# The end of a 31-tap convolution module: per-tile operand copies on two queues, squares summed on TensorE, and an earlier table load

## The reference, cut to what matters

```python
def conformer_conv(h, w1, b1, dw, dwb, ln_g, ln_b, w2, b2):
    u = h @ w1 + b1
    a, g = jnp.split(u, 2, axis=-1)
    u = a * jax.nn.sigmoid(g)
    u = dwconv(u, dw) + dwb          # depthwise, 31 taps
    u = jax.nn.silu(layernorm(u, ln_g, ln_b))
    return u @ w2 + b2
```

## Time and profile before

| what | value |
|---|---|
| time, median of 3 runs | 3130.01 us (3128.34 to 3136.8) |
| the profiled execution | 3120.8 us |
| its span | 3118.7 us |
| PE busy | 2922.0 us, 94% of the span |
| DVE, ACT, POOL busy | 65%, 38%, 12% |
| granted PE clock, mean | 0.97 |

### The profile page before, as it was taken

How to read it: one execution, slowest core, us unless ns; L and a number is a source line. 1 busy time by engine, 2 the same in 40 slices (tenths; PEclk the granted TensorE clock), 3 DMA queues, 4 the chain that set the end, 5 groups by cost and what they waited for, 6 DMA issues and landing times.

```text
span 3118.7 us, 41453 instructions
## 1 busy us (share of the span) xinstructions
PE 2922.0 (94%) x17128; PEld 2494.5 (80%) x17128; DVE 2011.5 (65%) x3228; ACT 1186.1 (38%) x1927; POOL 359.0 (12%) x540
## 2 busy tenths in 40 slices
PE   7998999889988989999998899999999999998898
PEld 7997899879977767888864578887887888787898
DVE  6776677758765657666663576667667664454665
ACT  5443444544443434333231442233224223343544
POOL 0000101000013221000122100001010000144000
PEclk9999999989989999999999899999999999999999
DMA  6544566436646543444455134443444442366453
GB/s 222 167 165 142 168 231 224 144 127 226 226 154 137 103 71 112 155 146 142 142 152 153 56 127 155 142 147 120 145 144 133 145 145 99 85 113 93 123 182 132
DMA packets 361756, 451.78 MB, mean 145 GB/s; under 512 B 12400, under 2 KB 332176, under 8 KB 361568
## 3 DMA queue, kind: packets, MB, share of 16 engines
q1 hardware_dynamic: 326208, 328.72, 32.2%
q0 software_dynamic: 35200, 119.82, 15.2%
q10 hardware_dynamic: 160, 0.59, 0.1%
HBM read 438.67 MB, written 1.05 MB: 141 GB/s over the span
## 4 chain that ended last, share of the span: by engine, by line
PE 77%; DVE 12%; ACT 5%; issue 3%; DMA 2%; POOL 1%; SPq 0%; DVEq 0%; ACTq 0%; POOLq 0%
PE ps L1011 23%; PE ps L1012 22%; PE ps L1013 22%; DVE MX L1533 2%; DVE lo L1479 2%; DVE lo L1482 2%; PE ps L1176 1%; ACT hi L1208 1%; PE ps L1167 1%; PE ps L1032 1%; PE ps L1034 1%; PE ps L1033 1%; DVE NB L1491 1%; DMA NB<-in_na_rpb 1%; PE ps L1076 1%
## 5 line engine op out<-in xcount | busy, mean ns | idle before, releaser
L1011 PE MATMUL ps<-XN,hi 128*128 128x256 f32 (+1 forms) x3008 | 1021.3, 340 | 80.4 <-DVE XN L1505 32.4
L1012 PE MATMUL ps<-XN,hi 128*128 128x256 f32 (+1 forms) x3008 | 1007.0, 335 | 0.0
L1013 PE MATMUL ps<-XN,lo 128*128 128x256 f32 (+1 forms) x3008 | 1006.3, 335 | 0.0
L1011 PEld LDWEIGHTS ps<-XN,hi 128*128 128x128 f32 x3008 | 582.5, 194 | 167.7 <-DVE XN L1505 39.7
L1013 PEld LDWEIGHTS ps<-XN,lo 128*128 128x128 f32 x3008 | 581.9, 193 | 54.5
L1012 PEld LDWEIGHTS ps<-XN,hi 128*128 128x128 f32 x3008 | 583.0, 194 | 52.8
L1479 DVE TENSOR_TENSOR lo<-raw,hi 128x1024 fp32r<-128x1024 f32 (+1 forms) x313 | 385.2, 1231 | 289.8 <-ACT hi L1208 288.0
L1533 DVE CUSTOM_DVE_ANT_0 MX<-MW,C 128x1024 bf16<-128x1024 f32 x384 | 485.7, 1265 | 41.0 <-DMA MW<-in_mod_w 34.3
L1208 ACT ACTIVATE hi<-raw 128x1024 fp32r<-128x1024 f32 (+1 forms) x313 | 326.1, 1042 | 440.7 <-PE ps L1013 436.4
L1482 DVE TENSOR_TENSOR lo<-raw,hi 128x1024 fp32r<-128x1024 f32 (+1 forms) x313 | 381.1, 1218 | 0.0
L1013 PE MATMUL ps<-H,lo 128*128 128x512 f32 (+1 forms) x1024 | 371.2, 363 | 0.0
(11 more groups left out here) (224 smaller groups left out, 3420.3 us busy)
## 6 DMA issues: line engine op xcount, KB each, us to landing
raw<-in_mlp_w SPq DMA_DIRECT2D x128, 1024.0 KB, 4.9
MW<-in_mod_w POOLq DMA_DIRECT2D x192, 512.0 KB, 3.8
raw<-in_ffn_w_in SPq DMA_DIRECT2D x44, 1024.0 KB, 5.0
raw<-in_attn_w_in SPq DMA_DIRECT2D x36, 1024.0 KB, 4.9
raw<-in_na_wqkv SPq DMA_DIRECT2D x24, 1024.0 KB, 5.7
raw<-in_ffn_w_out SPq DMA_DIRECT2D x16, 1024.0 KB, 5.1
raw<-in_mlstm_w_in SPq DMA_DIRECT2D x12, 1024.0 KB, 5.1
raw<-in_cv_w SPq DMA_DIRECT2D x12, 1024.0 KB, 5.6
```

What stands on the lines that cost most here:

```text
L1011: e.matmul(out, whi, xhi, start=first, stop=False)
L1012: e.matmul(out, whi, xlo, start=False, stop=False)
L1013: i = e.matmul(out, wlo, xhi, start=False, stop=last)
```

## The change

Three edits, all between the last product of the first matrix and the first product of the second one.

1. For c = 3 the step `cv_spread` is replaced by two steps `cv_spread_one`, one for tile 6 and one for tile 7, each right behind its `cv_a`. Each of them is carried out by two engines: POOL issues the copies of channel groups 0 and 1, SP those of groups 2 and 3, eight DMAs each, of 32 partitions x 572 columns. The convolutions of tiles 6 and 7 wait for the two halves of their own tile. Four semaphores are added.
2. The load of the logarithm and exponential table moves from behind convolution 7 to ahead of convolution 4.
3. `by_pool` goes from 2 to 1: POOL adds nothing, and PE takes in the squares of tiles 1 to 7 one by one.

```diff
         def evac_a(t, b, u):
             p.do("cv_a", 2 * c + t, t, b, u)
-            if t == 1:
+            if c == 3:
+                p.do("cv_spread_one", 6 + t)
+            elif t == 1:
                 p.do("cv_spread", c)
...
         for k in (2 * c - 2, 2 * c - 1):
             if k >= 0:
+                if k == KT - 4:
+                    p.do("tables", LNEXP)
                 convolve(k)
     for k in (KT - 2, KT - 1):
         convolve(k)
     p.sa_user = "cv_summed"
-    p.do("tables", LNEXP)
     p.do("cv_mean", p.bank_use[6], p.rs_user)
     for k in range(KT):
         p.do("cv_center", k, p.norms)
-        p.square(k, 512, 2, "CV")
+        p.square(k, 512, 1, "CV")
         p.flush()
...
+def spread_one(e, m, k, g, signal, name):
+    for i in range(4):
+        e.dma_start(m.UX[32 * i:32 * i + 32, k // 2 % 2, g, k % 2, 0:572],
+                    m.U[32 * g:32 * g + 32, k % 4, i:i + 572]).then_inc(*signal.says((name, k)))
...
 def sync(e, w, m, p, T, sig):
...
+    def cv_spread_one(k):
+        w.wait_ge(("cv_u", k), ("conv", 3))
+        for g in range(2, 4):
+            spread_one(e, m, k, g, sig[f"uxs{k}"], "uxs")
...
     def cv_conv(k, b, u):
-        w.wait_ge(("ux", k // 2), ("wd", k), free_of(b, u))
+        if k < KT - 2:
+            w.wait_ge(("ux", k // 2))
+        else:
+            w.wait_ge(("uxp", k), ("uxs", k))
+        w.wait_ge(("wd", k), free_of(b, u))
...
 def gpsimd(e, w, m, p, T, sig):
...
+    def cv_spread_one(k):
+        w.wait_ge(("cv_u", k), ("conv", 3))
+        for g in range(2):
+            spread_one(e, m, k, g, sig[f"ux{k}"], "uxp")
```

More of the change, by code:

```diff
@@ L155, in allocate @@
     m.sem = {n: ctx.enter_context(nc.semaphore(f"s_{n}"))
-             for n in ["acc", "act", "high", "dve", "low", "pool", "ld", "x0", "x1", "cond", "mw", "mm", "taps", "ux0", "ux1", "pv", "ci", "pos", "cst", "tb0", "tb1", "out"]
+             for n in ["acc", "act", "high", "dve", "low", "pool", "ld", "x0", "x1", "cond", "mw", "mm", "taps", "ux0", "ux1", "ux6", "ux7", "uxs6", "uxs7", "pv", "ci", "pos", "cst", "tb0", "tb1", "out"]
              + [f"raw{i}" for i in range(RAW)]}
@@ L994, in finish @@
         w.wait_ge(("stored", 1))
-    go_through(p, {"begin": begin, "load": load, "finish": finish})
+    go_through(p, {"begin": begin, "load": load, "cv_spread_one": cv_spread_one, "finish": finish})
 def tensor(e, w, m, p, acc):
@@ L1935, in gpsimd @@
     go_through(p, {"mod_load": mod_load, "square": square, "context": context, "ml_pads": ml_pads, "na_zero": na_zero,
-                   "na_table": na_table, "cv_pads": cv_pads, "cv_spread": cv_spread, "sc_pads": sc_pads})
+                   "na_table": na_table, "cv_pads": cv_pads, "cv_spread": cv_spread, "cv_spread_one": cv_spread_one,
+                   "sc_pads": sc_pads})
 def signals(m, table):
```

## The result

| | before | changed |
|---|---|---|
| median | 3129.18 us (3125.23 to 3136.8, 4 runs) | 3109.59 us (3105.93 to 3112.47, 4 runs) |
| profiled execution | 3120.8 us, span 3118.7 | 3106.95 us, span 3104.8 |

The ratio is 0.9939, with a 95% interval of 0.9923 to 0.9956: faster by 14 to 24 us, 19 by the middle. Forecast were 3112.5 us, 17.5 less, in a range of 3104 to 3122.

The account below looks back on a forecast made before the run. PE was taken to bound the kernel (77% of the span), with time won only where it stalls or runs at low clock. Terms 12.6 + 3.0 + 0.1 + 1.8 = 17.5 us off 3130.0 gave 3112.5 us, range 3104 to 3122.

Parts of the forecast that it names:

- The wait for tile 6's copies: Before convolution 6: copies issued from 1684.4 land before PE finishes convolution 5, so PE's 12.62 us wait goes; -12.6 us.
- The last rival: SP issues its copies slowly, 3.94 us each, so convolution 7 starts 24.3 us later; 3152.4 us, chance 0.03.
- the sign of being wrong: In the changed trace, SP's issues of the copies taking over a microsecond each would show the forecast wrong.
- The clock: Convolution 6, without the long gap ahead, runs at full clock: 9.95 us down to 7.0; -3.0 us, other end 0.
- Tile 7 in time: Before convolution 7: tile 7's copies land by 1709.9 to 1711.5, wanted at 1712.2; cost 0, other end 4.1 us.
- the first rival: SP's two weight loads slow tile 7's copies; convolution 7 starts 4.2 us late at low clock; 3119.7 us, chance 0.15.
- Cost per DMA, not per byte: Sixteen half-size copies take as long as full ones, 15.1 us; convolution 7 starts 3.0 us late; 3118.5 us, chance 0.09.
- The second queue: Splitting copies over POOL and SP saves POOL 4.3 us of issuing for tile 7, but moves data no faster.
- Table load: Before the mean on ACT: the moved load was hidden but for some 0.1 us; -0.1 us.
- Squares: After the mean: PE starts its sums 2.25 us earlier but makes eight instead of seven; -1.8 us (1.3 to 3.8).
- The sum: All terms together take 17.5 us off the span and median, with everything behind moving forward at unchanged lengths.

Follow-up runs that it names:

- e12: Kernel before with only the copies of tiles 6 and 7 changed (per tile, on POOL and SP); 3113.13 us, one run.
- e5: Changed kernel with POOL issuing all copies of tiles 6 and 7, tile by tile, SP none; median 3107.94 us, pooled with an identical kernel.
- e1: Changed kernel with tile 6's copies also issued only after the write of `U` 7, two queues and per-tile waits kept; 3121.47 us, ratio 0.9974.
- e11: Kernel before with only the logarithm and exponential table load moved; 3127.43 us, one run.
- e4: Kernel before with only the squares changed (`by_pool` 1, POOL adds nothing); 3129.20 us, one run.
- e6: Changed kernel with copies issued after the write of `U` 7, each DMA carrying both tiles, half the channel groups on SP; 3124.55 us, ratio 0.9992.
- e3: Changed kernel with SP issuing all copies of tiles 6 and 7, POOL none; 3115.88 us, one run.
- e7: Changed kernel with PE's sum over `SA` for tile 6 placed behind convolution 7 instead of ahead of it; 3105.64 us, one run.
- e10: The changed kernel itself, measured and profiled again in a later session; 3113.09 us, ratio 0.9950.
- e8: Changed kernel with DVE writing `U` of tile 7 ahead of the weight block of tile 6; 3111.72 us, one run.

## Why the prediction was right

*The wait for tile 6's copies, -12.6 us: right.* PE runs from convolution 5 into 6. e12 shows that edit 1 does it alone, and e5 that it needs no second queue; the wait per tile and the early start come together in both, and e1 puts the first at no more than 5.5 us. One number of the step was off: SP's eight copies were put at 3 to 5 us from other DMAs' rows and took 5.6 for tile 6 and 6.4 for tile 7. It did not matter, since tile 6's were there 10 us early. The last rival hung on this price. It needed a mean of 2.5 us an issue. The mean was 0.7 to 0.8, above the 0.37 to 0.60 of the other DMAs, and single issues took up to 1.85 us here and 2.59 in e12; so the sign of being wrong (over a microsecond each) came for single issues and not for the sixteen.

*The clock, -3.0 us: right for this pair of executions, high in general.* Convolution 6 behind the long wait took 9.95 us in the execution shown, but 8.67 in e11, 8.77 in e4, 9.25 in e6 and 9.73 in e1 (behind 7.42 us). Against 7.07 us its price is 1.6 to 2.9 us, and a single trace gave its top. That this term came out to the digit is luck in part: of the five executions with a long wait, the one that the forecast was read from has the longest convolution 6.

*Tile 7 in time, 0: right,* with 1.6 us to spare (0.7 to 2.3 were forecast from the earlier trace rows). SP issued the two weight loads from 1706.68 on, 2 to 4 us later than forecast, and they did not hold the copies up; the first rival did not come. e3 shows what it would have cost: the lateness, and the clock on top.

*Cost per DMA, not per byte:* the rival did not come. It wanted 15.1 us for sixteen half-size copies after the write of `U` 7, and e7 has them all after 10.3. Side by side in the same place, with both issuers and everything late, half-size copies landed in 4.6 us in the middle (e1) and full ones in 7.9 (e6, with the weight loads beside the last of them), so bytes count; but SP needs 0.66 to 1.05 us to issue each, and there the number of DMAs counts.

*The second queue:* said to save issue time alone. The engines at a share of 1.0 moved 226 GB/s with two issuers and 227 with one (e6, before). By the Trainium skill (DMA: Bandwidth & Descriptors, "Issuing engines are not separate DMA queues") several issuers do not add bandwidth, and these two rates agree. Of the 4.3 us of POOL's issue time that the prediction counted as saved nothing came off the module (18.43 us in e5 and with both): SP needs 6.44 us for its half of tile 7, POOL alone 7.82 for the whole, and the copies land later when both issue.

*Table load, -0.1 us: right,* 0.10 by e10 and e12.

*Squares, -1.8 us (1.3 to 3.8):* 1.5 in this pair, 2.1 in the mean over 13 readings. The range was too narrow below: e1 and e8 have 12.50 and 12.61, 0.2 to 0.3 under the row of before. The reckoning took before's 12.83 as fixed, but it moves with the clock as well (12.83 to 13.75). In the two executions of the changed kernel itself the clock fell at different points. The first sum of squares took 2.07 us in the row above and 1.13 in e10:

```profile
1720.25 1.13 PE L1055 MATMUL ps<-SA,cst 128*128 128x512 f32 x2 [2.07 <-ACT SA L1234]
```

The distance came out alike in both, 11.33 and 11.28; the 9.77 to 12.61 us are readings of kernels with the same code for the squares that differ elsewhere. The Trainium skill (TensorE: Matmul & The Clock Gate, "What's actually happening") says that the point at which the clock changes varies from run to run, and the two first sums agree with it.

*The sum, 17.5 us:* 17.3 in the module in this pair. Over all executions it is about 17.0: the first distance is 33.3 us in the mean of the three that wait for all copies from one queue (before, e4, e11) and 18.4 in the changed kernel, 14.9 us, and the squares give 2.1. So the clock's term was some 0.9 us high (33.3 against the 34.2 of the pair) and the squares' 0.3 low, and they made up for each other in part. The step from the module to the whole time assumed that everything behind moves forward unchanged. In work it does; the lengths behind scatter by some 3 us from one execution to the next, whichever kernel it is. The medians' 19 us (14 to 24) and e10's ratio (0.9950, 16 us) hold 17 between them.

## What to carry to other kernels

When an engine waits for the last of a batch of transfers, look at when the first item of the batch was ready; moving each item as soon as it is written, with its own wait, was worth nine tenths of this change. A second issuing queue was worth nothing, and giving all copies to the slower issuer (SP) cost 2.6 us. Once a wait is gone, ask whether anything else still stands between the two pieces of work: here one small sum in PE's order cost another 2.8 us, and the copies' slack of 1.6 us had to be widened first. Price a phase that starts behind a short idle time from several executions, since the same code took 9.8 to 12.6 us here. And when a move puts other transfers behind the ones under test, look at what they move in the same time before reading the wait, as in e6.

## What the runs showed of the hardware that was not expected

- Issuing one SBUF-to-SBUF DMA of 32 partitions cost SP 0.51 to 2.59 us (the longest in e12), in rows of eight or sixteen 0.66 to 1.05 on average (10.54/16 in e1, 6.44/8, 11.24/16 in e3, 8.43/8 in e6), where POOL took 0.49 to 0.54. SP's own weight loads take 0.37 us alone, and 0.63 to 0.71 right behind such copies (1.26 to 1.41 for two).
- Copies of the same size landed later when two engines issued them: tile 7's in 4.5 us in the middle with both (changed kernel), 2.6 with POOL alone (e5), 2.1 with SP alone (e3); tile 6's in 2.7, 2.1 and 2.0.
- A DMA share of 1.0 was not a fixed rate: 250 GB/s with copies of 2.3 KB rows in the mix, and 319 GB/s, at the same share, while weight loads took over from them (1707 to 1713 in the changed kernel).
- In e3 PE stood between convolutions 6 and 7 for 3.5 us, with 1.1 us of work in the middle, and convolution 7 began at the low clock (0.51 from 1721.5 to 1725) and took 8.76 us. In the ten executions with 2.6 us there, with the same work in it, it took 7.07.
